# Low probability halves converted by VectorE, and gate work, stores and weight loads rescheduled, in a fused attention stage

## The chip, the cores and the metric

The kernel runs on one core of one Trainium2 chip. The metric is device time in microseconds of one execution, here the median of several runs. One execution was also recorded by the hardware profiler, and all durations below come from that one.

## The reference, cut to what matters

```python
z = einsum('bsd,de->bse', x, w_in) + b_in          # one projection, 2048 tokens x 1024
y_a = pool_mixer(za, ...) * silu(ga)
y_b = fox_attention(zq, zk, zv, zf) * silu(gb)     # 8 heads of 64, causal, forget-gate bias
y_c = s5_mixer(zc, ...) * silu(gc)
gates = sigmoid(zg)                                 # 3 x 1024 channels
merged = sum of gates[n] * (y_n @ w_up_n)
out = layer_norm(alpha * x + merged @ w_out)
# fox_attention, for each block of 128 queries:
logits = where(mask, q @ k.T * scale + F[t] - F[s], -inf)
y = softmax(logits) @ v
```

## The kernel before

Three stages follow each other: the input projections, scans and pooling; `stage_attend`; and the lifting and output projections. The change touches `stage_attend` alone, and the table `fill_plan` that it uses.

Products in this kernel are made of float32 operands split into a high part (rounded to the matmul's format) and a low part (the remainder); two or three matmuls then stand for one. `stage_attend` runs eight heads, one after the other, and mixes two kinds of work.

**Attention of a head**, by 16 tiles t of 128 queries. PE multiplies queries with all keys up to the tile's end into five PSUM banks `s_ps` (`queries`, L1819 and L1820). DVE subtracts the forget-gate row and takes the row maximum (`logits`, L1715, L1729). ACT makes the exponential (`weights_of`, L1636) and a float16 high half `p_hi` (`high_halves`, L1644); DVE makes the low half `p_lo` (L1783), in chunks of up to 1024 keys. A tile t of 8 or more has two chunks, so a head has 24. SP sends each half through a transposing DMA into `turn_hi` and `turn_lo` (L1467, L1471). ACT converts `turn_hi` to `pt_hi` (`high_turned`, L1649), POOL converts `turn_lo` to `pt_lo` (`low_turned`, L1534). PE then multiplies both with the values, two query tiles (a pair p) at a time (`values`, L1836), ACT copies half of the result (`low_rows`, L1607) and DVE adds it (`output`, L1738).

**Gates.** Beside that, PE computes the sigmoid gates for half of the tokens per four heads: each head has 6 weight tiles x 2 column chunks = 12 pieces of 24 matmuls (`fill`, L1866), 288 in all. Weight tiles come from HBM (L1392, issued by SP), are split by ACT (L1590) and DVE (L1699), the result goes through a tanh on ACT (`gates`, L1601) and is stored to `gateT` by SP (L1459).

What sets the order: each engine's program is written out by hand, with semaphores between them. `fill_plan` says how many of the 288 gate matmuls PE puts into each slot: "start" (ahead of or just behind the head's first query products), slot t behind the query products of tile t+1, "end" ahead of the last `values(7)`, and "tail" behind it. It also says in which slot a piece ends, and in which slot a weight tile is split. SP's queue holds the transposes of tile t and then the gate stores and weight loads of slot t; a wait there holds up all that stands behind it. POOL's queue holds the low-half conversions, the stores of each pair, and the loads of the next head: `load_kq` (four of 512 KB) at tile 15, `load_f` (1 MB), `load_v` (1 MB).

The lines that set the pace on PE before:

```python
for t in range(Q_TILES):
    if t + 1 < Q_TILES:
        queries(at, t + 1)
    fill(t)
    if t % 2 == 0 and t >= 2:
        values(at, t // 2 - 1, final)
fill("end")
values(at, 7, final)
fill("tail")
```

Of the kernel before, what the change touches and what calls it, by code (L numbers as in the profile page):

```python
# [1254 lines left out]
def fill_plan():  # L1255
# [32 lines left out]
FILL_START, FILL_END, FILL_TAIL, FILL_BASE = 30, 16, 22, 5  # L1288
# [16 lines left out]
def chunks_to(t):  # L1305

    return chunks(t)[-1][0] + 1


def stage_attend(nc, io, scr, kept, ident, mask, x_hi, x_lo, x_raw, gw_hi, gw_lo, gw_raw):  # L1310
# [4 lines left out]
    with ExitStack() as ctx:  # L1315
# [68 lines left out]
        assert nc.sbuf_base <= kept.wu_at + 4 * KT * KT * P  # L1384
        block = ctx.enter_context(nc.Block())

        @block.sync
        def _(sp):
            w_rows = io["w_tiles"].rearrange("m p (k c) -> (m p) k c", c=P)

            def load_w(first_row, par):
                sp.dma_start(gw_raw[par][:], w_rows[bass.ds(first_row, P)]).then_inc(gw_loaded[par], 16)  # L1392

# [5 lines left out]
            load_w((T_HALF + 1) * P, 1)  # L1399
# [38 lines left out]
            def body(phase, at, in_phase, last=False, turn=False):  # L1438
                now = (1 - phase) * HALF

                def gate_pieces(slot):
                    for piece in fill_ends[slot]:
# [19 lines left out]
                def transposes(t):  # L1462
                    for n, b0, nb in chunks(t):
# [3 lines left out]
                        sp.dma_start_transpose(turn_hi[n % 2][:, 0:nb, :], p_hi[n % 2][:, 0:nb * P]).then_inc(hi_turned[n % 2], 16)  # L1467
                        sp.wait_ge(p_low, at(CHUNKS_HEAD, n + 3))
# [4 lines left out]
                gate_pieces("start")  # L1473
                for t in range(Q_TILES):
# [3 lines left out]
                    gate_pieces(t)  # L1478
# [13 lines left out]
        def _(pool):  # L1492
# [33 lines left out]
            def low_turned(at, t):  # L1526

                if t >= 2 and t % 2 == 0:
                    pool.wait_ge(o_full, at(8, t // 2))
                    pool.sem_inc(passed)  # L1530
                for n, b0, nb in chunks(t):
                    pool.wait_ge(lo_turned[n % 2], at(CHUNKS_HEAD * 8, 16 * (n // 2) + (turned + 16)))
                    pool.sem_inc(passed)
                    pool.tensor_scalar(pt_lo[:, b0:b0 + nb, (t % 2) * P:(t % 2 + 1) * P], turn_lo[n % 2][:, 0:nb, :],  # L1534
                                       1.0 / HALVES, None, ALU.mult).then_inc(t_lo, 1)

            def tiles(at, row, last=False):
# [20 lines left out]
            with pool.Fori(0, HEADS - 1) as h:  # L1558
# [6 lines left out]
                low_turned(of_head, Q_TILES - 1)  # L1565
# [5 lines left out]
            low_turned(lambda k, c: (HEADS - 1) * k + c, Q_TILES - 1)  # L1571
# [14 lines left out]
        def _(act):  # L1586
# [5 lines left out]
            def gates(at, in_phase, slot, last=False):  # L1592
                for j in splits(slot, last):
                    split_w(at, j)
                for piece in fill_ends[slot]:
# [6 lines left out]
                                   bias=g_bias[:, bass.ds(in_phase(G_TILES, j), 1)]).then_inc(g_ready, 1)  # L1602

# [28 lines left out]
            def body(at, in_phase, last=False, turn=False):  # L1632
# [24 lines left out]
                gates(at, in_phase, "start", last)  # L1657
                for t in range(Q_TILES):
                    if t:
                        weights_of(t)  # L1660
                        if t % 2 and t >= 3:
                            low_rows(at, (t - 3) // 2)
                        before, now = chunks(t - 1), chunks(t)
# [799 lines left out]
```

## Time and profile before

| what | us |
|---|---|
| median of 3 runs (2101.03 to 2112.96) | 2109.07 |
| the profiled execution's own time | 2108.43 |
| its span | 2106.9 |
| PE busy in the span | 1825.6 (87%) |
| DVE, ACT, POOL busy | 1134.8, 833.9, 858.3 |
| DMA queue of SP, mean share of the 16 engines | 45.3% |
| DMA queue of POOL, the same | 11.4% |

Busy shares are means over stages with different limits. A row of a group tells the idle time of its engine just ahead of it and what ended that. PE's own durations overlap (matmuls are pipelined), so its pace is read from the distance between starts. The granted clock is given as a share of 2.4 GHz; 0.50 is 1.2 GHz.

### The profile page before, as it was taken

What the parts mean: (1) busy time and instruction counts of PE and PEld (TensorE: products, weight loads), DVE (VectorE), ACT (ScalarE), POOL (GpSimd) and SP (SyncE); (2) the same over time, 40 slices, a digit from 0 to 9 for tenths busy, and PEclk for the clock granted to TensorE, in tenths of its full rate; (3) what the DMA queues carried; (4) which work ended last, traced back from release to release, by engine and by line L of the source; (5) the groups of instructions that cost most, each with busy time, mean ns of one, the idle gap of its engine ahead of it and who ended that gap; (6) DMA issues with size and microseconds to landing.
All of it is one profiled execution on the core that took longest, in us unless ns stands there. A gap on an engine that the chain in (4) does not pass through costs nothing. (4 is left out here: it accounts for less than half of the span.)

```text
span 2106.9 us, 30302 instructions
## 1 busy us (share of the span) xinstructions
PE 1825.6 (87%) x9469; PEld 1556.6 (74%) x9469; DVE 1134.8 (54%) x2293; ACT 833.9 (40%) x1184; POOL 858.3 (41%) x778
## 2 busy tenths in 40 slices
PE   9999999999988689588596786886886889999998
PEld 7988888988866567566475565675665778999997
DVE  4555254653455346256264563462653658777766
ACT  3122131121255547356265564473663563121211
POOL 2919801990015425335155254253362451323232
PEclk9999999999999899789799898998998999999999
DMA  7322343323446747747668578477575788656652
GB/s 213 108 82 87 126 176 100 121 90 112 145 118 133 159 116 154 159 110 155 138 141 171 188 140 164 117 150 168 114 167 146 164 217 283 198 170 171 186 152 90
DMA packets 408628, 310.65 MB, mean 147 GB/s; under 512 B 304377, under 2 KB 354105, under 8 KB 405177
## 3 DMA queue, kind: packets, MB, share of 16 engines
q1 hardware_dynamic: 390576, 243.45, 45.3%
q0 software_dynamic: 15152, 63.06, 11.4%
q10 hardware_dynamic: 2800, 2.99, 0.6%
q8 instruction: 41, 0.67, 0.1%
q14 instruction: 59, 0.48, 0.1%
HBM read 164.05 MB, written 73.47 MB: 113 GB/s over the span
## 5 line engine op out<-in xcount | busy, mean ns | idle before, releaser
L1534 POOL TENSOR_SCALAR pt_lo<-turn_lo 128x1024 fp32r<-128x1024 f16 (+2 forms) x192 | 405.3, 2111 | 500.1 <-DMA turn_lo<-p_lo 411.8
L1836 PE MATMUL o_ps<-pt_hi,v_st 128*128 128x256 f32 x576 | 166.8, 319 | 224.0 <-POOL pt_lo L1534 208.2
L1836 PEld LDWEIGHTS o_ps<-pt_hi,v_st 128*128 128x128 f32 x576 | 128.6, 223 | 249.3 <-issue 249.2
L1866 PE MATMUL g_ps<-x_hi,w_hi 128*128 128x512 f32 x768 | 304.7, 397 | 0.0
L1866 PE MATMUL g_ps<-x_hi,w_lo 128*128 128x512 f32 x768 | 304.2, 396 | 0.0
L1715 DVE CUSTOM_DVE_ANT_0 s_sb<-s_ps,f_row 128x512 f32<-128x512 f32 (+3 forms) x288 | 160.1, 598 | 198.9 <-PE s_ps L1820 198.6
L1866 PE MATMUL g_ps<-x_lo,w_hi 128*128 128x512 f32 x768 | 233.0, 431 | 38.6 <-DVE w_lo L1699 37.4
L1783 DVE SCALAR_TENSOR_TENSOR p_lo<-s_sb,p_hi 128x1024 f16<-128x1024 f32 (+2 forms) x192 | 192.0, 1018 | 118.0 <-ACT p_hi L1644 111.6
L1866 PEld LDWEIGHTS g_ps<-x_lo,w_hi 128*128 128x128 f32 x768 | 157.4, 210 | 75.0 <-issue 32.4
L1649 ACT ACTIVATE pt_hi<-turn_hi 128x1024 fp32r<-128x1024 f16 (+2 forms) x192 | 154.1, 802 | 91.9 <-DMA turn_hi<-p_hi 91.8
L1636 ACT ACTIVATE s_sb<-s_sb,neg_max 128x128 f32<-128x128 f32 (+15 forms) x128 | 153.1, 1196 | 46.6 <-DVE neg_max L1729 46.4
L1866 PEld LDWEIGHTS g_ps<-x_hi,w_hi 128*128 128x128 f32 x768 | 148.1, 193 | 29.8
L1866 PEld LDWEIGHTS g_ps<-x_hi,w_lo 128*128 128x128 f32 x768 | 147.5, 192 | 29.9
L904 PE MATMUL tile_ps<-x_hi,w_hi 128*128 128x512 f32 x528 | 164.6, 393 | 0.2 <-DVE w_lo L511 0.2
L904 PE MATMUL tile_ps<-x_hi,w_lo 128*128 128x512 f32 x528 | 162.8, 389 | 0.0
L904 PE MATMUL tile_ps<-x_lo,w_hi 128*128 128x512 f32 x528 | 162.6, 389 | 0.0
L1836 PE MATMUL o_ps<-pt_lo,v_st 128*128 128x256 f32 x576 | 159.2, 313 | 0.0
L1699 DVE TENSOR_TENSOR w_lo<-w_lo_raw,w_hi 128x1024 fp32r<-128x1024 f32 x47 | 57.5, 1224 | 183.8 <-ACT w_hi L1590 183.8
L1644 ACT ACTIVATE p_hi<-s_sb 128x1024 f16<-128x1024 f32 (+2 forms) x192 | 151.7, 794 | 0.0
L2290 PE MATMUL u_ps<-y_hi,wu_hi 128*128 128x256 f32 x512 | 144.2, 282 | 4.2 <-DVE gate L2215 2.3
L2290 PE MATMUL u_ps<-y_lo,wu_hi 128*128 128x256 f32 x512 | 144.5, 282 | 0.0
L2290 PE MATMUL u_ps<-y_hi,wu_lo 128*128 128x256 f32 x512 | 143.8, 281 | 0.0
(333 smaller groups left out, 3845.3 us busy)
## 6 DMA issues: line engine op xcount, KB each, us to landing
w_lo_raw<-in_w_tiles SPq DMA_DIRECT2D x87, 512.0 KB, 4.2
gateT<-g_out SPq DMA_DIRECT2D x96, 256.0 KB, 4.2
gate<-gateT SPq DMA_DIRECT2D x62, 384.0 KB, 4.7
x_lo_raw<-in_xT SPq DMA_DIRECT2D x20, 512.0 KB, 9.7
vS<-v_out SPq DMA_DIRECT2D x32, 256.0 KB, 2.0
silT<-zout SPq DMA_DIRECT2D x16, 512.0 KB, 2.6
qkvT<-zout SPq DMA_DIRECT2D x16, 512.0 KB, 3.6
k_ll<-qkvT POOLq DMA_DIRECT2D x16, 512.0 KB, 8.1
```

Source lines behind the costliest of these rows:

```text
L904: last = pe.matmul(tile_ps[par][:, c * BANK:(c + 1) * BANK], w[par][:, k, :], x[:, k, c * BANK:(c + 1) * BANK], start=(k == 0 and j == 0), ...
L1534: pool.tensor_scalar(pt_lo[:, b0:b0 + nb, (t % 2) * P:(t % 2 + 1) * P], turn_lo[n % 2][:, 0:nb, :], 1.0 / HALVES, None, ALU.mult).then_inc ...
L1636: act.activation(row, row, ACT.Exp, bias=neg_max[t % 2][:], accum_out=row_sum[:, t:t + 1]).then_inc(p_ready, 1)
L1644: act.activation(p_hi[n % 2][:, 0:nb * P], s_sb[t % 2][:, b0 * P:(b0 + nb) * P], ACT.Copy, scale=HALVES).then_inc(p_high, 1)
L1649: act.activation(pt_hi[:, b0:b0 + nb, (t % 2) * P:(t % 2 + 1) * P], turn_hi[n % 2][:, 0:nb, :], ACT.Copy, scale=1.0 / HALVES).then_inc(t_h ...
L1699: dve.tensor_tensor(gw_lo[j % 2][:], gw_raw[j % 2][:], gw_hi[j % 2][:].bitcast(F32), ALU.subtract).then_inc(gw_split, 1)
L1715: return dve.tensor_tensor_reduce(s_sb[t % 2][:, k0 + a:k0 + b], s_ps[n % S_BANKS][:, a:b], f, 1.0, -3e38, ALU.subtract, ALU.max, mx[t % 2 ...
L1783: dve.scalar_tensor_tensor(p_lo[n % 2][:, 0:nb * P], s_sb[t % 2][:, b0 * P:(b0 + nb) * P], HALVES, p_hi[n % 2][:, 0:nb * P], ALU.mult, ALU ...
L1836: mm = pe.matmul(o_ps[:, 0, q], v_st[:, k, :], pt[:, k, q], start=(k == 0 and j == 0), stop=(k == last_key and j == 1))
L1866: mm = pe.matmul(g_ps[c][:], w[j % 2][:, k, :], x[:, k, c * BANK:(c + 1) * BANK], start=(r == 0), stop=(r == 3 * KT - 1))
L2290: mm = pe.matmul(u_ps[d % 2][:, n, :], w, y[:, k, :], start=(k == k0 and j == 0), stop=(k == k1 - 1 and j == 2))
```

## The change

1. `low_turned` moves from POOL to DVE. It is done one tile later, chunk by chunk: in the iteration of tile t, DVE converts chunk i of tile t-1 behind `p_lo` of chunk i of tile t. POOL keeps only DMAs.
2. ACT makes `high_halves` of tile t ahead of `high_turned` of tile t-1, and the tanh of slot t-1 moves into the iteration of tile t, behind the exponential.
3. The weight loads are issued by ACT, behind the tanh of the piece that frees the buffer, in place of SP. Weight splits stand in the middle of a tile, behind its first chunk; at the head's end they stand behind the split of the next head's keys and queries.
4. SP stores the gates of slot t-1 between the first high and the first low transpose of tile t.
5. PE starts `values(p)` behind `queries` of tile 2p+4 in place of behind `fill` of tile 2p+2, and does all products with `pt_hi` first; it waits for `t_lo` only ahead of those with `pt_lo`.
6. The gate matmuls of a head are 14 (start), 8, 10, 10, 11, 12, 13, 13, 14, 15, 15, 16, 17, 18, 18, 20, 20 (slots 0 to 15), 30 (end), 14 (tail). Before: 30, then 5, 7, 7, 9, 10, 11, 12, 13, 15, 15, 17, 17, 19, 20, 21, 22, then 16 and 22.

```diff
-FILL_START, FILL_END, FILL_TAIL, FILL_BASE = 30, 16, 22, 5
+FILL_START, FILL_END, FILL_TAIL, FILL_BASE = 14, 30, 14, 12
-                at = s + (3 if s < 4 else 2)
+                at = s + (3 if s < 12 else 2)
...
@@ SP, transposes(t)
-                    for n, b0, nb in chunks(t):
+                    for i, (n, b0, nb) in enumerate(chunks(t)):
...
                         sp.dma_start_transpose(turn_hi[n % 2][:, 0:nb, :], p_hi[n % 2][:, 0:nb * P]).then_inc(hi_turned[n % 2], 16)
+                        if i == 0:
+                            gate_pieces(t - 1 if t else "start")
...
@@ ACT, body
+                for t in range(1, Q_TILES):
+                    weights_of(t)
+                    gates(at, in_phase, t - 1, last, turn)
+                    before = chunks(t - 1)
+                    for i, part in enumerate(chunks(t)):
+                        high_halves(t, *part)
+                        if i == 0:
+                            if t % 2 and t >= 3:
+                                low_rows(at, (t - 3) // 2)
+                            for j in splits(t, last):
+                                split_w(at, j)
+                        if i < len(before):
+                            high_turned(t - 1, *before[i])
...
@@ DVE
+            def low_turned(at, t, n, b0, nb):
+                dve.wait_ge(lo_turned[n % 2], at(CHUNKS_HEAD * 8, 16 * (n // 2) + (turned + 16)))
+                dve.sem_inc(passed)
+                dve.tensor_scalar(pt_lo[:, b0:b0 + nb, (t % 2) * P:(t % 2 + 1) * P], turn_lo[n % 2][:, 0:nb, :],
+                                  1.0 / HALVES, None, ALU.mult).then_inc(t_lo, 1)
...
@@ DVE, body, behind p_lo of chunk i of tile t
+                        if i == 0:
+                            if t % 2 and t >= 3:
+                                output(at, (t - 3) // 2, last)
+                            for j in splits(t, last):
+                                split_w(at, j)
+                        if i < len(before):
+                            low_turned(at, t - 1, *before[i])
...
@@ PE, values
-                for part in (t_hi, t_lo):
-                    pe.wait_ge(part, at(CHUNKS_HEAD, chunks_to(2 * p + 1) + 2))
+                pe.wait_ge(t_hi, at(CHUNKS_HEAD, chunks_to(2 * p + 1) + 2))
...
+                for j, pt in enumerate((pt_hi, pt_lo)):
+                    if j:
+                        pe.wait_ge(t_lo, at(CHUNKS_HEAD, chunks_to(2 * p + 1) + 2))
...
@@ PE, head
+                        if t % 2 and t >= 3:
+                            values(at, (t - 3) // 2, final)
                         fill(t)
-                        if t % 2 == 0 and t >= 2:
-                            values(at, t // 2 - 1, final)
```

DVE at the end of a head, in the kernel before (`pt_lo` does not occur on it):

```order
572 L1783 SCALAR_TENSOR_TENSOR p_lo<-s_sb,p_hi 128x1024
573 L1780 REGISTER_ALU
574 L1783 SCALAR_TENSOR_TENSOR p_lo<-s_sb,p_hi 128x1024
575 L1787 RECIPROCAL row_inv<-row_sum 128x16
576 L1698 REGISTER_ALU
577 L1699 TENSOR_TENSOR w_lo<-w_lo_raw,w_hi 128x1024
```

The same place in the kernel after:

```order
592 L1779 SCALAR_TENSOR_TENSOR p_lo<-s_sb,p_hi 128x1024
593 L1730 REGISTER_ALU
594 L1731 REGISTER_ALU
595 L1733 TENSOR_TENSOR y_out_108<-o_ps,o_low 64x256
596 L1687 REGISTER_ALU
597 L1688 TENSOR_TENSOR w_lo<-w_lo_raw,w_hi 128x1024
598 L1724 TENSOR_SCALAR pt_lo<-turn_lo 128x8x128
599 L1776 REGISTER_ALU
600 L1779 SCALAR_TENSOR_TENSOR p_lo<-s_sb,p_hi 128x1024
601 L1724 TENSOR_SCALAR pt_lo<-turn_lo 128x7x128
602 L1790 RECIPROCAL row_inv<-row_sum 128x16
603 L1722 REGISTER_ALU
```

The conversions of tile 14 now stand between and behind the two `p_lo` of tile 15; the pair's sum and a weight split stand ahead of the first of them.

PE around `values(1)`, before (four key tiles; `s_ps` are the query products that follow):

```order
1812 L1826 REGISTER_ALU
1813 L1830 ISA
1814 L1836 MATMUL o_ps<-pt_hi,v_st 128x256
1815 L1836 MATMUL o_ps<-pt_lo,v_st 128x256
1816 L1836 MATMUL o_ps<-pt_hi,v_st 128x256
1817 L1836 MATMUL o_ps<-pt_lo,v_st 128x256
...
1822 L1817 REGISTER_ALU
1823 L1819 MATMUL s_ps<-k_hh,q_st 128x512
1824 L1820 MATMUL s_ps<-k_ll,q_st 128x512
```

After:

```order
1809 L1820 MATMUL s_ps<-k_hh,q_st 128x512
1810 L1821 MATMUL s_ps<-k_ll,q_st 128x512
...
1816 L1838 MATMUL o_ps<-pt_hi,v_st 128x256 x3
1817 L1838 MATMUL o_ps<-pt_hi,v_st 128x128
1818 L1838 MATMUL o_ps<-pt_lo,v_st 128x256 x3
1819 L1838 MATMUL o_ps<-pt_lo,v_st 128x128
1820 L1868 MATMUL g_ps<-x_hi,w_lo 128x512
```

The next tile's query products have moved ahead of the value products, and the high ones stand ahead of the low ones.

SP at the end of a head, before:

```order
249 L1467 DMA_TRANSPOSE turn_hi<-p_hi 128x8x128
250 L1468 REGISTER_ALU
251 L1471 DMA_TRANSPOSE turn_lo<-p_lo 128x8x128
252 L1467 DMA_TRANSPOSE turn_hi<-p_hi 128x8x128
253 L1468 REGISTER_ALU
254 L1471 DMA_TRANSPOSE turn_lo<-p_lo 128x8x128
255 L1392 ISA
256 L1392 DMA w_lo_raw<-in_w_tiles 128x1024
```

After:

```order
237 L1461 DMA_TRANSPOSE turn_hi<-p_hi 128x8x128
238 L1452 REGISTER_ALU
239 L1453 ISA
240 L1453 DMA gateT<-g_out_106 128x512
241 L1464 REGISTER_ALU
242 L1467 DMA_TRANSPOSE turn_lo<-p_lo 128x8x128
243 L1461 DMA_TRANSPOSE turn_hi<-p_hi 128x8x128
244 L1464 REGISTER_ALU
245 L1467 DMA_TRANSPOSE turn_lo<-p_lo 128x8x128
```

A gate store now stands ahead of the first low transpose of tile 15, and the weight load has left the queue.

## Rows read from the trace of the kernel before

**Rows 1.** Windows by stage: stretch, length, busy by engine, clock, DMA share, GB/s
```profile
0.00:595.00 595.00, 588.22 (x3056) 498.00 (x3056) 299.48 (x336) 128.11 (x150) 283.45 (x378) 1.00 0.37 122
595.00:1735.00 1140.00, 878.46 (x4106) 731.65 (x4107) 563.62 (x1454) 626.15 (x897) 476.00 (x306) 0.89 0.67 150
1735.00:2106.90 371.90, 358.95 (x2309) 326.95 (x2307) 271.73 (x504) 79.66 (x138) 98.81 (x94) 0.99 0.60 180
```

**Rows 2.** Groups by line: busy us, mean ns of one, idle before, releaser
```profile
L1534 POOL TENSOR_SCALAR pt_lo<-turn_lo 128x1024 fp32r<-128x1024 f16 (+2 forms) x192 | 405.3, 2111 | 500.1 <-DMA turn_lo<-p_lo 411.8 <-PE o_ps L1836 83.1
...
L1866 PE MATMUL g_ps<-x_lo,w_hi 128*128 128x512 f32 x768 | 233.0, 431 | 38.6 <-DVE w_lo L1699 37.4 <-PEq L1891 1.2
...
L1836 PE MATMUL o_ps<-pt_hi,v_st 128*128 128x256 f32 x576 | 166.8, 319 | 224.0 <-POOL pt_lo L1534 208.2 <-issue 15.8
```

**Rows 3.** PE's timeline, one head: all its rows that begin behind a wait
```profile
907.89 0.58 PE L1836 MATMUL o_ps<-pt_hi,v_st 128*128 128x256 f32 x1 [6.65 <-POOL pt_lo L1534]
927.55 0.57 PE L1836 MATMUL o_ps<-pt_hi,v_st 128*128 128x256 f32 x1 [2.67 <-POOL pt_lo L1534]
941.09 0.38 PE L1836 MATMUL o_ps<-pt_hi,v_st 128*128 128x256 f32 x1 [0.22 <-POOL pt_lo L1534]
955.58 0.38 PE L1836 MATMUL o_ps<-pt_hi,v_st 128*128 128x256 f32 x1 [2.37 <-POOL pt_lo L1534]
971.34 0.38 PE L1836 MATMUL o_ps<-pt_hi,v_st 128*128 128x256 f32 x1 [1.65 <-POOL pt_lo L1534]
988.26 0.38 PE L1836 MATMUL o_ps<-pt_hi,v_st 128*128 128x256 f32 x1 [0.86 <-POOL pt_lo L1534]
998.82 3.65 PE L1866 MATMUL g_ps<-x_lo,w_hi 128*128 128x512 f32 x8 [4.21 <-DVE w_lo L1699]
1024.15 0.58 PE L1836 MATMUL o_ps<-pt_hi,v_st 128*128 128x256 f32 x1 [17.55 <-POOL pt_lo L1534]
```

**Rows 4.** PE's timeline at full clock: gate matmuls, sixteen starts
```profile
597.16 0.40 PE L1866 MATMUL g_ps<-x_hi,w_hi 128*128 128x512 f32 x1
...
600.57 0.39 PE L1866 MATMUL g_ps<-x_hi,w_lo 128*128 128x512 f32 x1
```

**Rows 5.** `turn_lo` in 990 to 1025 us, and windows in that head's end
```profile
DMA to landing us min/median/max: 2.9/3.3/22.5
...
1000.00:1005.00 5.00, 5.00 (x19) 4.02 (x18) 0.00 (x0) 1.06 (x1) 3.91 (x4) 0.78 1.00 209
...
1015.00:1020.00 5.00, 0.00 (x0) 0.00 (x0) 0.00 (x0) 0.00 (x0) 0.00 (x0) 0.50 1.13 88
```

**Rows 6.** Windows: the head of Rows 3, from key split to key split
```profile
878.70:1025.60 146.90, 110.72 (x515) 92.48 (x515) 67.72 (x178) 77.34 (x110) 58.63 (x39) 0.86 0.65 140
```

**Rows 7.** POOL's and SP's timelines around the end of that head
```profile
997.95 0.56 POOL L1495 DMA_DIRECT2D k_ll<-qkvT  x1
...
1000.57 0.58 POOL L1502 DMA_DIRECT2D f_row<-fcum  x1
...
1021.15 2.76 POOL L1534 TENSOR_SCALAR pt_lo<-turn_lo 128x1024 fp32r<-128x1024 f16 x1 [17.16 <-DMA turn_lo<-p_lo]
...
998.50 1.23 SPq L1471 DMA_TRANSPOSE turn_lo<-p_lo  x1
```

**Rows 8.** Groups by form: conversions on three engines
```profile
L1534 POOL TENSOR_SCALAR pt_lo<-turn_lo 128x1024 fp32r<-128x1024 f16 x80 | 224.3, 2804 | 274.7 <-DMA turn_lo<-p_lo 194.3 <-PE o_ps L1836 79.7
L771 DVE TENSOR_SCALAR m_in<-zf 8x2048 f32<-8x2048 f32 x1 | 1.2, 1206 | 0.0
L691 DVE TENSOR_SCALAR pool_u<-tile_ps,bias 128x1024 f32<-128x1024 f32 x4 | 5.1, 1284 | 9.8 <-PE tile_ps L904 9.8
```

**Rows 9.** DVE's timeline, tile 15 of that head: first logits, first low half of tile 14
```profile
981.53 0.69 DVE L1715 CUSTOM_DVE_ANT_0 s_sb<-s_ps,f_row 128x512 f32<-128x512 f32 x1 [0.73 <-PE s_ps L1820]
...
984.52 1.23 DVE L1783 SCALAR_TENSOR_TENSOR p_lo<-s_sb,p_hi 128x1024 f16<-128x1024 f32 x1
```

**Rows 10.** A DMA issued by ACT's queue
```profile
25.31 0.34 ACTq L258 DMA_DIRECT2D vb_lo_raw<-in_w_vf  x1
```

More of the change, by code:

```diff
@@ L1477, in body @@
                     transposes(t)
-                    gate_pieces(t)
+                gate_pieces(Q_TILES - 1)
                 if last:
@@ L1590, in split_w, with gates @@
                 act.activation(gw_hi[j % 2][:], gw_raw[j % 2][:], ACT.Copy).then_inc(gw_split_hi, 1)
-            def gates(at, in_phase, slot, last=False):
-                for j in splits(slot, last):
-                    split_w(at, j)
+            def gates(at, in_phase, slot, last=False, turn=False):
                 for piece in fill_ends[slot]:
@@ L1602, in gates @@
                                    bias=g_bias[:, bass.ds(in_phase(G_TILES, j), 1)]).then_inc(g_ready, 1)
+                    if c == NCH - 1 and not (last and j + 2 >= G_TILES):
+                        if turn and j + 2 >= G_TILES:
+                            load_w(act, (T_HALF + j + 2 - G_TILES) * P, j % 2)
+                        else:
+                            load_w(act, in_phase(G_TILES * P, (T_HALF + j + 2) * P), j % 2)
             def low_rows(at, p):
@@ L1656, in body @@
                     high_halves(0, *part)
[L1657 to L1663, printed above, removed]
-                        for i in range(len(now)):
-                            if i < len(before):
-                                high_turned(t - 1, *before[i])
-                            high_halves(t, *now[i])
-                    gates(at, in_phase, t, last)
+                gates(at, in_phase, "start", last, turn)
+                for t in range(1, Q_TILES):
[11 more added lines that the diff above has]
+                            high_turned(t - 1, *before[i])
+                gates(at, in_phase, Q_TILES - 1, last, turn)
                 for part in chunks(Q_TILES - 1):
@@ L1676, in body @@
                         high_wu(i)
-                gates(at, in_phase, "end", last)
+                else:
+                    split_kq(at(64, 128))
+                for j in splits("end", last):
+                    split_w(at, j)
+                gates(at, in_phase, "end", last, turn)
                 if last:
@@ L1688, in body @@
                     high_x(0)
-                gates(at, in_phase, "tail", last)
+                gates(at, in_phase, "tail", last, turn)
                 if turn:
@@ L1778, in body @@
                         logits(at, t + 1)
-                    for n, b0, nb in chunks(t):
+                    before = chunks(t - 1) if t else []
+                    for i, (n, b0, nb) in enumerate(chunks(t)):
                         dve.wait_ge(p_high, at(CHUNKS_HEAD, n + 1))
@@ L1787, in body @@
                         dve.reciprocal(row_inv[:, 0:t + 1], row_sum[:, 0:t + 1]).then_inc(inv_ready, 1)
-                    for j in splits(t, last):
-                        split_w(at, j)
-                    if t % 2 and t >= 3:
-                        output(at, (t - 3) // 2, last)
-                for j in splits("end", last):
-                    split_w(at, j)
+                for part in chunks(Q_TILES - 1):
+                    low_turned(at, Q_TILES - 1, *part)
                 if last:
@@ L1799, in body @@
                     split_kq(at(2, 4))
+                for j in splits("end", last):
+                    split_w(at, j)
                 output(at, 7, last)
@@ L1831, in values @@
                 last_key = 2 * p + 1
-                for k in range(last_key + 1):
-                    q = slice(P, 2 * P) if k == last_key else slice(0, 2 * P)
-                    for j, pt in enumerate((pt_hi, pt_lo)):
+                for j, pt in enumerate((pt_hi, pt_lo)):
+                    if j:
+                        pe.wait_ge(t_lo, at(CHUNKS_HEAD, chunks_to(2 * p + 1) + 2))
+                    for k in range(last_key + 1):
+                        q = slice(P, 2 * P) if k == last_key else slice(0, 2 * P)
                         mm = pe.matmul(o_ps[:, 0, q], v_st[:, k, :], pt[:, k, q], start=(k == 0 and j == 0),
```

30 lines of the change are left out of this document (5 added, 25 removed).

## The prediction

> **What bounds the kernel now.** First I read the windows by stage [rows 1]. Ahead of 595 us and behind 1735 us PE is busy 588.2 of 595.0 and 359.0 of 371.9 us at a clock of 1.00 and 0.99: the change touches neither, and there is nothing for it to win. In the attention stage between them PE is busy 878.5 of 1140 us at a mean clock of 0.89. So 261.5 us are idle, 32.7 in each of the eight heads, and a head takes 142.5. The groups by line then say what ends that idle time: value products waiting for POOL's conversion of the low halves, 224.0 us in all, and gate products waiting for a weight split, 37.4 [rows 2]. PE's timeline of one head shows where [rows 3]: 6.7 us ahead of the first value product, 0.2 to 2.7 ahead of the next five, 4.2 ahead of the gate products of the last weight tile, and 17.6 ahead of the last value product. That is 32.0 of waits for low halves in this head; the mean over the heads is 224.0 / 8 = 28, so the others are like it and somewhat shorter, above all in the last wait (the last head loads nothing for a next one).
>
> How much work is in a head? 15 steps between gate matmuls of 512 columns take 3.41 us, 0.227 each [rows 4]. So 288 of them are 65.5 us. The query products have 136 x 128 keys twice, 34,816 columns, and the value products 128 x 256 + 16 x 128, as many: at the gates' pace per column 15.4 us each. Together 96.3 us at full clock. PE is busy 878.5 / 8 = 109.8, so 13.5 us a head are lost to the low clock: behind long waits it is granted 0.50 [rows 5], and the eight gate matmuls behind the wait at 998.82 take 3.65 us [rows 3] in place of 8 x 0.227 = 1.8. **A head is 96.3 work + 13.5 slow clock + 32.7 idle.** No other engine is near: in a head of 146.9 us DVE is busy 67.7, ACT 77.3, POOL 58.6 [rows 6].
>
> POOL is named as releaser, but it was itself waiting for the transposing DMA, 411.8 us [rows 2]. At the head's end it issued the loads of the next head's keys and queries (2 MB) from 997.95 and the gate row (1 MB) at 1000.57. SP issued the last low transpose at 998.50, and it landed after 22.5 us, where the median is 3.3; the DMA engines were fully busy meanwhile [rows 5, 7]. So of the 17.6 us POOL's own arithmetic is 2.8, and the rest is that collision. This wait is half of a head's idle time, and what becomes of it decides the size of the result.
>
> **The change, part by part.**
>
> *The conversion on DVE.* POOL takes 2.80 us for 1024 keys [rows 8]. The trace has no such operation on DVE. Nearest is a one-operand instruction with both tiles in SBUF, 2048 in 1.21 us (0.59 ns per column); an upper bound is one that reads PSUM, 1024 in 1.28 (1.25 ns) [rows 8]. A head has 17,408 columns: 10.3 to 21.8 us. I take 12, by the row it is like. DVE goes to 67.7 + 12 = 80 us a head, 90 at worst: below PE's 96. For the last pair of chunks 2 x 2.8 us on POOL become 2 x 0.7.
>
> *First value product, 6.7 us.* The chain from the first row maximum to the converted tile 1 loses POOL's small conversions and a store that stood ahead of the first transpose, but stays some 9 us of exponential, halves and transposes. Ahead of it PE now has 28 gate matmuls in place of 19 (8 + 10 + 10 for 5 + 7 + 7), +2.0 us, and the query products of tile 4, +0.6. I leave 3, bounds 1 and 6.
>
> *The next ones up to pair 6*, 7.8 us in this head. Queries of the next tile now stand ahead of the wait, so DVE gets its input while PE waits, and half of the products (those with `pt_hi`) need no low half. Between the query products of an even tile and the values PE has 1.8 + 4.5 + 1.8 us late in the head (0.227 x 2 per 512 keys, 20 gate matmuls); DVE needs 3.0 (logits) [rows 9], 2.4 (two `p_lo` of 1.23 at most) and 1.4 (conversions). That fits, with 1 to 2 us over. I leave 2, bounds 0 and 8.
>
> *Weight splits, 4.2 us.* The last tile's split comes earlier in tile 15, and PE reaches it with matmul 240, late in slot 15. But tile 3's split now stands in tile 10 and PE wants it 9 matmuls into that slot, where DVE has logits and a `p_lo` ahead of it: 2 us, bounds 0 and 4. ACT issues 6 loads a head, 0.34 us each [rows 10]: 2 us on an engine that has 60 free. SP loses them, and loses their wait for PE.
>
> *Last value product, 17.6 us (some 14 in a mean head).* Two effects, opposed. POOL no longer lags, so it issues the 2 MB as soon as tile 15's query products are done, about 14 us earlier: those were done by 981.53, where DVE starts on tile 15 [rows 9]. They then run beside the transposes of tile 14 and the first of tile 15, and the 1 MB beside the rest. The sum of bytes is the same, and a load begun 14 us earlier ends that much earlier; but more transposes are in its way. From the start of tile 15's query products PE now has these 1.8, 20 gate matmuls 4.5, `values(6)` 3.2, again 20 gates 4.5 and the 30 of "end" 6.8: 21 us. The chain needs: 2 MB at 209 GB/s [rows 5] 10 us (from +2), then tile 15's halves and transposes, an estimate of 10 (three landings of 3.3), and the 1 MB 5: about +28. Before, the last values began 42 us behind that point. I leave 7, bounds 0 and 15. The Trainium skill, page "DMA: Bandwidth & Descriptors", section "Queues, rings and completion order", says that each DMA engine takes turns between queues packet by packet. This trace agrees as far as it goes: the one transpose that shared the DMA engines with POOL's loads took 22.5 us to land, 19 more than the median. By it the early load would slow four to six transposes, not two, and the wait would stay: the first rival below.
>
> *Slow clock.* Of four to five waits over 2 us a head, two stay. 13.5 becomes 7, bounds 2 and 11.
>
> *Reordering of ACT, SP stores a tile later, and the even spread of gates* cost nothing by themselves: the work is the same, and ACT at 79 and SP's queue stay below PE: that work hides them. If PE came near 100 us a head this cover would be thin, since DMA work is 0.65 x 146.9 = 95 us a head [rows 6].
>
> Sum: 96.3 + 3 + 2 + 2 + 7 + 7 = 117.3 us a head, 25.2 less than 142.5. Eight heads give 202 us. The last head has no load of a next head to collide with and so less to win; I take off 8: 194. From the profiled execution's 2108.4 us: **1914 us**. That execution lies 0.6 below the median of the runs, so no correction.
>
> **The rivals.**
>
> *A. The collision stays.* The wait at the head's end keeps 15 us and the clock loss 9: 127.3 + 1 for thinner cover, 128.3 a head, 14.2 x 8 = 114 less, 1994 us. For it: the landing of 22.5 us and DMA at 1.00 to 1.13 [rows 5]. Against it: the loads start earlier, and 12 to 14 more gate matmuls stand ahead.
>
> *B. DVE becomes the bound late in the head.* If the conversion costs 1.28 per 1024, tiles 10 to 15 need some 8 us of DVE each (3.0 + 2.4 + 2.5), with a weight split over that, and DVE holds the pace: 1.3 us for each of six tiles, +8 a head, 1978 us. For it: the order, a landing now waited for by DVE with the next logits queued behind. Against: DVE's total of 90 at worst.
>
> *C. Slower: two serial landings.* DVE and ACT now wait in order for tile 14's transposes between the two chunks of tile 15. If tile 14's transposes crawl under the 2 MB load (19 us more than 3.3) and then tile 15's under the 1 MB and the stores (19 us more), the chain holds two collisions in place of one: a wait of 15 + 19, clock 12: 96.3 + 3 + 2 + 2 + 34 + 12 = 149.3 a head, +6.8, 2162 us. It decides if the two delays together exceed some 33 us. Against: DMA work of all those bytes is about 30 us, so both can't be full.
>
> *D. No gain.* POOL's lag was harmless and each wait returns with another releaser, within 0.5% (10 us, about what a measurement of this kernel can tell from no change): 2108. Against: the conversion is 2.8 us of every wait, and PE's order alone removes some.
>
> *E. Nearly all goes.* Wait at the end 2, first 1, others 1, clock 4: 96.3 + 8 = 104.3 a head, 38 less in each of seven and 12 in the last, 1830 us, since the load ends before PE gets there.
>
> **How the numbers follow.** Forecast 0.48, A 0.19, B 0.10, E 0.14, C 0.05, D 0.04. Faster: 0.91, same 0.04, slower 0.05. The range 1835 to 2025 holds the forecast with its bounds, A and B with 30 us over, and half of E; it leaves out C, D and the rest of E.
>
> **What would show it.** In the new profile POOL has no busy group in the stage; the conversion on DVE is 0.6 to 0.8 us for 1024 keys (B: 1.2 or more). PE's busy time in the stage falls from 878 to about 830, the clock rises to 0.93 or more, and idle time from 262 to about 110. The wait ahead of the last value product is 4 to 10 us (A: 13 or more, C: 25 or more) and is ended by DVE's conversion behind a landing. The row of the last weight tile's wait is gone, and a smaller one may stand in slot 10. The forecast is wrong if PE's waits between pairs 1 and 6 grow, or if key loads lengthen the landings of tile 14 so that the last wait keeps its length.

## The result, and the profile after

The changed kernel takes 1989.3 us (median of three, 1986.6 to 2016.0), against 2109.1 before: a ratio of 0.948, interval 0.934 to 0.961. It is faster by 120 us, where 194 were forecast (1914 us); the range held it. Since its own three runs span 29 us, a difference of 20 us to it is read below together with the traces. The profiled execution has a span of 1985.0 us against 2106.9, 121.9 less.

The attention stage in the windows of the kernel after; the columns are those of [rows 1]:

```profile
596.00:1614.00 1018.00, 857.02 (x4109) 715.56 (x4109) 649.37 (x1646) 635.69 (x898) 74.63 (x114) 0.93 0.76 168
```

All the gain is here: 1140 us became 1018, 127.3 a head. PE's busy time fell from 878.5 to 857.0 (about 830 were forecast) and its idle time from 261.5 to 161.0 (110 were forecast). POOL is all but empty, DVE grew from 564 to 649.

The groups by line, the answer to [rows 2]:

```profile
L1868 PE MATMUL g_ps<-x_lo,w_hi 128*128 128x512 f32 x768 | 230.9, 430 | 95.3 <-DVE w_lo L1688 91.4
...
L1779 DVE SCALAR_TENSOR_TENSOR p_lo<-s_sb,p_hi 128x1024 f16<-128x1024 f32 (+2 forms) x192 | 175.1, 912 | 115.2 <-DMA turn_lo<-p_lo 97.1
...
L1628 ACT ACTIVATE p_hi<-s_sb 128x1024 f16<-128x1024 f32 (+2 forms) x192 | 154.0, 802 | 132.8 <-DMA turn_hi<-p_hi 123.1
...
L1838 PE MATMUL o_ps<-pt_hi,v_st 128*128 128x256 f32 x576 | 80.2, 285 | 47.9 <-ACT pt_hi L1633 47.9
```

The value products waited 224.0 us before and now 57 (47.9, and 9.3 ahead of the low ones). The wait for weight splits grew from 37.4 to 91.4 and is now the largest. And two waits are new: ACT's high half and DVE's low half wait for the landing of the transpose that frees their buffer, 123.1 and 97.1 us. ACT's high half did not wait before. DVE's low half stood idle as long, but for ACT:

```profile
L1783 DVE SCALAR_TENSOR_TENSOR p_lo<-s_sb,p_hi 128x1024 f16<-128x1024 f32 (+2 forms) x192 | 192.0, 1018 | 118.0 <-ACT p_hi L1644 111.6 <-issue 1.8
```

PE's timeline of one head, the answer to [rows 3], with all rows that begin behind a wait:

```profile
865.45 0.68 PE L1838 MATMUL o_ps<-pt_hi,v_st 128*128 128x256 f32 x2 [5.60 <-ACT pt_hi L1633]
866.78 0.69 PE L1838 MATMUL o_ps<-pt_lo,v_st 128*128 128x256 f32 x2 [0.65 <-DVE pt_lo L1724]
907.13 2.36 PE L1868 MATMUL g_ps<-x_lo,w_hi 128*128 128x512 f32 x7 [3.01 <-DVE w_lo L1688]
931.70 2.11 PE L1868 MATMUL g_ps<-x_lo,w_hi 128*128 128x512 f32 x8 [1.51 <-DVE w_lo L1688]
943.16 1.88 PE L1838 MATMUL o_ps<-pt_lo,v_st 128*128 128x256 f32 x14 [0.44 <-DVE pt_lo L1724]
955.33 3.78 PE L1868 MATMUL g_ps<-x_lo,w_hi 128*128 128x512 f32 x8 [6.56 <-DVE w_lo L1688]
966.55 2.12 PE L1838 MATMUL o_ps<-pt_hi,v_st 128*128 128x256 f32 x16 [1.24 <-ACT pt_hi L1633]
974.44 2.10 PE L1868 MATMUL g_ps<-x_lo,w_hi 128*128 128x512 f32 x8 [0.56 <-DVE w_lo L1688]
```

The waits of pairs 1 to 6 are all but gone, and the last one fell from 17.6 to 1.2. In their place stand the splits of weight tile 3 (3.0), 4 (1.5) and, above all, 5 (6.6). In the seven heads that load for a next one, the wait for tile 5's split is 2.5 to 12.2 us.

Around that last split, on POOL, SP, ACT and DVE:

```profile
937.28 0.52 POOL L1490 DMA_DIRECT2D k_ll<-qkvT  x1 [5.00 <-PE s_ps L1821]
...
940.60 9.01 SPq L1467 DMA_TRANSPOSE turn_lo<-p_lo  x1
...
951.11 1.06 ACT L1628 ACTIVATE p_hi<-s_sb 128x1024 f16<-128x1024 f32 x1 [8.53 <-DMA turn_hi<-p_hi]
...
952.52 1.23 DVE L1779 SCALAR_TENSOR_TENSOR p_lo<-s_sb,p_hi 128x1024 f16<-128x1024 f32 x1 [9.42 <-DMA turn_lo<-p_lo]
...
954.00 1.21 DVE L1688 TENSOR_TENSOR w_lo<-w_lo_raw,w_hi 128x1024 fp32r<-128x1024 f32 x1
...
964.49 0.69 DVE L1724 TENSOR_SCALAR pt_lo<-turn_lo 128x1024 fp32r<-128x1024 f16 x1 [6.39 <-DMA turn_lo<-p_lo]
```

The 2 MB load begins at 937.28, right behind tile 15's query products. From there tile 14's transposes crawl: SP needs 9.01 us to issue one of them (1.2 else), and ACT and DVE stand still for 8.5 and 9.4 us. The weight split is behind them in DVE's order, so PE, which does not need the transposes for another 11 us, waits for the split. **The collision at the head's end is still there; it moved from tile 15's transposes to tile 14's, and its stall reaches PE by another way.** That the load is its cause is shown by the first experiment below.

The conversion by form on DVE:

```profile
L1724 DVE TENSOR_SCALAR pt_lo<-turn_lo 128x1024 fp32r<-128x1024 f16 x80 | 54.9, 687 | 65.1 <-DMA turn_lo<-p_lo 65.0
...
L1724 DVE TENSOR_SCALAR pt_lo<-turn_lo 128x896 fp32r<-128x896 f16 x16 | 17.2, 1072 | 0.0
```

1024 keys take 0.69 us, as taken in the sum. All 192 take 117.6 us, 14.7 a head; 12 were forecast, and the odd sizes like 896 make the difference.

### The profile page after: what moved, and what is told of

It is laid out like the page before. It is cut to its first block and busy times, and to the rows that moved or that the text cites. A ratio compares the mean times of both kernels' runs of the same rounds, so it can differ in the third digit from the quotient of the medians.

```text
span 1985.0 us, 30017 instructions
## 1 busy us (share of the span) xinstructions
PE 1805.1 (91%) x9469; PEld 1542.0 (78%) x9469; DVE 1223.3 (62%) x2485; ACT 842.4 (42%) x1184; POOL 455.8 (23%) x586
## 3 DMA queue, kind: packets, MB, share of 16 engines
q0 software_dynamic: 15152, 63.06, 12.0%
## 5 line engine op out<-in xcount | busy, mean ns | idle before, releaser
L1868 PE MATMUL g_ps<-x_lo,w_hi 128*128 128x512 f32 x768 | 230.9, 430 | 95.3 <-DVE w_lo L1688 91.4
L1868 PE MATMUL g_ps<-x_hi,w_hi 128*128 128x512 f32 x768 | 310.4, 404 | 0.0
L1868 PE MATMUL g_ps<-x_hi,w_lo 128*128 128x512 f32 x768 | 308.7, 402 | 0.0
L1779 DVE SCALAR_TENSOR_TENSOR p_lo<-s_sb,p_hi 128x1024 f16<-128x1024 f32 (+2 forms) x192 | 175.1, 912 | 115.2 <-DMA turn_lo<-p_lo 97.1
L1511 POOL DMA_DIRECT2D mixT<-y_out x63 | 40.1, 636 | 852.5 <-DVE y_out L1733 698.7
L1628 ACT ACTIVATE p_hi<-s_sb 128x1024 f16<-128x1024 f32 (+2 forms) x192 | 154.0, 802 | 132.8 <-DMA turn_hi<-p_hi 123.1
L1724 DVE TENSOR_SCALAR pt_lo<-turn_lo 128x1024 fp32r<-128x1024 f16 (+2 forms) x192 | 117.6, 613 | 106.9 <-DMA turn_lo<-p_lo 106.5
L1868 PEld LDWEIGHTS g_ps<-x_hi,w_hi 128*128 128x128 f32 x768 | 149.3, 194 | 30.3
L375 ACT ACTIVATE w_hi<-w_lo_raw 128x1024 fp32r<-128x1024 f32 x39 | 41.3, 1058 | 195.1 <-DMA w_lo_raw<-in_w_tiles 195.1
L1838 PE MATMUL o_ps<-pt_hi,v_st 128*128 128x256 f32 x576 | 80.2, 285 | 47.9 <-ACT pt_hi L1633 47.9
L1820 PE MATMUL s_ps<-k_hh,q_st 128*128 128x512 f32 (+2 forms) x320 | 120.1, 376 | 3.9 <-DVE q_st L1750 2.7
```

The source lines that it names most:

```text
L1628: act.activation(p_hi[n % 2][:, 0:nb * P], s_sb[t % 2][:, b0 * P:(b0 + nb) * P], ACT.Copy, scale=HALVES).then_inc(p_high, 1)
L1724: dve.tensor_scalar(pt_lo[:, b0:b0 + nb, (t % 2) * P:(t % 2 + 1) * P], turn_lo[n % 2][:, 0:nb, :], 1.0 / HALVES, None, ALU.mult).then_inc( ...
L1779: dve.scalar_tensor_tensor(p_lo[n % 2][:, 0:nb * P], s_sb[t % 2][:, b0 * P:(b0 + nb) * P], HALVES, p_hi[n % 2][:, 0:nb * P], ALU.mult, ALU ...
L1820: pe.matmul(ps, q_st[:, t * P:(t + 1) * P], k_hh[:, k0:k0 + keys], start=True, stop=False)
L1838: mm = pe.matmul(o_ps[:, 0, q], v_st[:, k, :], pt[:, k, q], start=(k == 0 and j == 0), stop=(k == last_key and j == 1))
L1868: mm = pe.matmul(g_ps[c][:], w[j % 2][:, k, :], x[:, k, c * BANK:(c + 1) * BANK], start=(r == 0), stop=(r == 3 * KT - 1))
```

## The experiments

Each was run beside the kernel before on the same chip; its ratio is to that kernel. The theory has three parts. The 2 MB load collides with whichever transposes are in flight. A weight split that PE waits for costs what that wait shows. The place of the value products and the engine of the conversion share the gain. Rivals are in each expectation. Parts 2 and 4 of the change (ACT's order and the later stores of the gates) and the place of the splits within a tile (part 3) were not taken out by themselves.

| run | us | ratio to before, interval |
|---|---|---|
| the change | 1989.3 | 0.948, 0.934 to 0.961 |
| e1 split a slot earlier | 1968.3 | 0.933, 0.930 to 0.937 |
| e2 key load later | 2007.0 | 0.951, 0.948 to 0.953 |
| e3 key load tiny | 1931.2 | 0.914, 0.911 to 0.917 |
| e4 last split early | 1988.4 | 0.943, 0.939 to 0.947 |
| e5 old fill counts and split slots | 1969.7 | 0.932, 0.928 to 0.937 |
| e6 conversion on POOL | 2051.2 | 0.972, 0.965 to 0.978 |
| e7 old value order | 2048.7 | 0.970, 0.966 to 0.973 |
| e8 before, conversion on DVE | 2074.6 | 0.981, 0.978 to 0.985 |
| e9 e1, head split later | 1962.7 | 0.929, 0.926 to 0.932 |
| e10 e1, queries loaded early | 1999.5 | 0.944, 0.941 to 0.948 |
| e11 e9 and e10 | 1992.9 | 0.942, 0.939 to 0.946 |
| e12 weights loaded by SP | 2000.9 | 0.946, 0.943 to 0.950 |

### The load at the head's end

```diff
@@ e3, load_kq (q_st alike)
-pool.dma_start(k_ll[half], scr["qkvT"][q_row + D_B ...])
+pool.dma_start(k_ll[half, 0:P], scr["qkvT"][q_row + D_B ..., 0:P])
```

> The change, but of the next head's keys and queries only 128 columns are loaded (128 KB in place of 2 MB), so heads 1 to 7 work on wrong keys and queries. Theory: the landings of tile 14's transposes return to 3 us, DVE and ACT do not stall, the wait at the last weight tile falls from 6.5 to under 1, that of the last value product stays under 3: 7 x 9 = 63 us less than the change, about 1922. Rival (DVE's own order at the end sets that wait): within 15 us of the change, and the row of the last weight tile's wait stays over 4 us.

1931.2 us: 58 less than the change (63 expected). DVE's timeline of this run at tile 15's first low half, then PE's at the last value product:

```profile
929.65 1.23 DVE L1779 SCALAR_TENSOR_TENSOR p_lo<-s_sb,p_hi 128x1024 f16<-128x1024 f32 x1 [2.10 <-DMA turn_lo<-p_lo]
```
```profile
945.55 3.67 PE L1838 MATMUL o_ps<-pt_hi,v_st 128*128 128x256 f32 x16 [4.15 <-ACT pt_hi L1633]
```

DVE's stall there fell from 9.4 to 2.1 us and the row of the last weight tile's wait is gone, as expected; the last wait did not stay under 3, it is 4.2. The gate row's 1 MB is still loaded while tile 15's transposes are in flight; whether it makes this wait was not tested. So the 2 MB load costs 8 us in each of seven heads, and the theory holds against DVE's order as the cause.

```diff
@@ e2: load_kq from tile 15's start to just ahead of load_f
-                        load_kq(row + HD)
+                pool.wait_ge(s_full, h * S_PIECES + S_PIECES)
+                load_kq(h * HD + HD)
                 pool.wait_ge(s_free, h * S_PIECES + S_PIECES)
                 load_f(h + 1)
```

> The change, but the 2 MB of keys and queries of the next head are loaded behind the store of pair 6, together with the gate row, some 17 us later. Theory (the 2 MB crawl over whichever transposes are in flight): the wait of 6.5 us at the last weight tile goes to under 1, DVE's stall of 9 us on tile 14's landing goes, and the wait of the last value product grows from 1.5 to 12 to 16; 7 x 5 = 35 us slower than the change, about 2020. Rival (where the load stands does not matter, bytes are bytes): within 10 us of the change. Second rival (the early load is a loss of its own): 30 us or more faster.

2007.0 us, 18 more than the change by the medians (35 expected); the intervals overlap (0.948 to 0.953 and 0.934 to 0.961). PE's timeline of this run, the last value product, and the landings of its low transposes:

```profile
848.42 3.67 PE L1837 MATMUL o_ps<-pt_hi,v_st 128*128 128x256 f32 x16 [12.83 <-ACT pt_hi L1632]
```
```profile
DMA to landing us min/median/max: 2.2/3.0/30.3
```

The wait is back in its old place, 12.8 us, and the longest landing is 30.3. In the seven heads that load, this wait is 14.8 us on average; in the change, the wait for tile 5's split and the last one are 8.8 together. Over the profiled executions PE is idle for 207.8 us here and 179.9 in the change. So the traces show the early load of the change as the better of the two places, though neither is free; by the times alone that is not settled.

```diff
@@ e4, fill_plan
-                at = s + (3 if s < 12 else 2)
+                at = s + (1 if s == 13 else 3 if s < 12 else 2)
```

> The change, but the last weight tile (5) is split in slot 14 in place of 15. Theory (the chain of transposes to the last value product is what counts, and the wait at the weight tile only stands in its shadow): the 6.5 us wait at the weight tile goes and the wait of the last value product grows by about as much, to 7 to 8; time within 10 us of the change. Rival (the weight split is itself the limit): 7 x 6 = 42 us less, about 1945.

1988.4 us, the change's time, as expected. PE's timeline of this run:

```profile
961.25 2.12 PE L1868 MATMUL g_ps<-x_lo,w_hi 128*128 128x512 f32 x8 [1.74 <-ACT g_out L1580]
...
971.61 3.58 PE L1838 MATMUL o_ps<-pt_hi,v_st 128*128 128x256 f32 x16 [7.77 <-ACT pt_hi L1633]
```

The 6.6 us at the weight tile became 1.7 (now behind ACT's stalled tanh) and the last value product's 1.2 became 7.8. The largest row of the profile after was a shadow: what counts there is when tile 15's transposes land.

```diff
@@ e10: load_kq keeps k_ll and the last quarter of q_st; POOL, behind the store of a pair
+                        if t in (5, 9, 13) and not last:
+                            pool.wait_ge(s_full, at(S_PIECES, pieces_to(t)))
+                            load_q(row + HD, t // 4 - 1)
```

> As e1, and three quarters of the next head's queries are loaded at tiles 5, 9 and 13, where their columns are free, so that 1.25 MB in place of 2 MB are loaded at tile 15. Theory (the price of that load is in proportion to what is loaded beside tile 14's transposes; all of it costs 54 us by e3): 0.75 / 2 of 54 = 20 us less than e1, 1948, with shorter waits at value product 6 and 7. Rival (the same bytes cost the same wherever they meet transposes): within 6 us of e1.

1999.5 us: 31 more than e1, where 20 less were expected. This misses the theory's forecast that the price goes by the bytes at tile 15. DVE's timeline of this run, late in a head:

```profile
939.65 1.23 DVE L1787 SCALAR_TENSOR_TENSOR p_lo<-s_sb,p_hi 128x1024 f16<-128x1024 f32 x1 [3.14 <-DMA turn_lo<-p_lo]
...
947.13 1.09 DVE L1787 SCALAR_TENSOR_TENSOR p_lo<-s_sb,p_hi 128x896 f16<-128x896 f32 x1 [5.65 <-DMA turn_lo<-p_lo]
...
968.05 0.69 DVE L1732 TENSOR_SCALAR pt_lo<-turn_lo 128x1024 fp32r<-128x1024 f16 x1 [10.24 <-DMA turn_lo<-p_lo]
```

The quarter at tile 13 begins 2.3 us ahead of the rest, and the stall is spread over three chunks and is no shorter. The price does not go by bytes at tile 15. The run also has more packets on POOL's queue for the same 63.06 MB (16,720 for 15,152), since rows are cut in four; whether the cut rows or the earlier start made it slower was not told apart. e11 adds the head split of e9 to it:

> e9 and e10 together. Theory: the two are at different places of the head and add up, 35 us less than e1, 1933. Rival: less than half of that, 1950 or more.

1992.9 us: more than e9 alone (1962.7) and within 7 us of e10, so its rival (1950 or more) holds and the two do not add up.

### The splits and the counts

```diff
@@ e1, fill_plan
-                at = s + (3 if s < 12 else 2)
+                at = s + (3 if s < 4 else 2)
```

> The change, but the weight tiles 3, 4 are split in slots 9 and 12, as in the kernel before, in place of 10 and 13. Theory (PE paces tiles 2 to 13 and waits there only for these splits): the waits of 3.0 and 1.3 us a head at the gate products of tiles 3 and 4 go, with some slow clock, 8 x 4.5 = 36 us less than the change, about 1953. Rival (DVE paces these tiles, so that the time returns in another wait, or the weight load has not landed and ACT waits for it): within 10 us of the change.

1968.3 us, 21 less than the change (36 expected); all four runs (1960.3 to 1975.9) lie below the change's three. PE's timeline of this run, tiles 9 to 15 of a head: the rows of the weight tiles 3 and 4 are gone, and

```profile
942.08 3.25 PE L1838 MATMUL o_ps<-pt_lo,v_st 128*128 128x256 f32 x14 [4.55 <-DVE pt_lo L1724]
950.25 2.11 PE L1868 MATMUL g_ps<-x_lo,w_hi 128*128 128x512 f32 x8 [0.24 <-DVE w_lo L1688]
962.05 3.67 PE L1838 MATMUL o_ps<-pt_hi,v_st 128*128 128x256 f32 x16 [3.79 <-ACT pt_hi L1633]
```

PE now reaches the collision earlier and gives part back there: 4.6 and 3.8 us, 8.6 in all with the split, where the change had 8.2. That the time fell shows that PE does pace the tiles up to 13, and the rival (DVE paces them) falls.

```diff
@@ e5
-FILL_START, FILL_END, FILL_TAIL, FILL_BASE = 14, 30, 14, 12
+FILL_START, FILL_END, FILL_TAIL, FILL_BASE = 30, 16, 22, 5
-                at = s + (3 if s < 12 else 2)
+                at = s + (3 if s < 4 else 2)
```

> The change with the old counts of gate matmuls (30 at the start, 16 end, 22 tail, steep in between) and the old slots of the splits. Theory (the even spread gives PE work ahead of the first and the last value product, where the chain of transposes ends late): the wait of the first value product grows by 2 us, that of the last by 3 to 8 (14 gate matmuls fewer ahead of it, and no wait at the weight tile to hide in), less 20 us for the splits as seen when they alone were a slot earlier: 15 to 50 us slower than the change, about 2015. Rival (the counts only shift idle time): within 10 us of the change, or faster by the 20 us of the splits.

1969.7 us: 20 less than the change, and the time of e1, which has the same split slots with the new counts. The theory falls and the rival's second form holds: with the old split slots the even spread of the gate products is worth nothing that can be measured. PE's groups of this run show why:

```profile
L1868 PE MATMUL g_ps<-x_lo,w_hi 128*128 128x512 f32 x768 | 229.9, 426 | 40.2 <-DVE w_lo L1688 35.7 <-ACT g_out L1580 2.4 <-PEq L1893 1.2
L1838 PE MATMUL o_ps<-pt_lo,v_st 128*128 128x256 f32 x576 | 91.8, 311 | 36.3 <-DVE pt_lo L1724 36.3
L1838 PE MATMUL o_ps<-pt_hi,v_st 128*128 128x256 f32 x576 | 89.0, 306 | 60.0 <-ACT pt_hi L1633 60.0
```

The three waits are 132 us; in e1 the same three are 130 (8.0 + 40.7 + 81.2). The counts only decide on which of them the collision falls.

```diff
@@ e9, fill_plan, on top of e1
-    splits["head"] = [1]
+    splits["head"], splits[1] = [], [1]
```

> As e1 (splits of tiles 3, 4 a slot earlier), and the split of weight tile 1 stands in slot 1 in place of the head's first steps, where it lies between the first and the second logits. Theory (the wait ahead of the first value product, 3.5 us in a mean head of e1 with its low part, is the chain exponential, halves, transposes of tiles 0 and 1, and 2.8 us of it are this split on ACT and DVE): 1.5 to 2.8 us a head less, 1950 against e1's 1968. Rival (SP's issue of the first transpose, or the landing, sets it): within 6 us of e1.

1962.7 us, 6 less than e1, which is what the rival allows, and the intervals overlap (0.926 to 0.932 and 0.930 to 0.937). The theory's 12 to 22 us did not come. PE's timeline, the first value product of a head, first of e1, then of e9:

```profile
986.00 0.44 PE L1838 MATMUL o_ps<-pt_hi,v_st 128*128 128x256 f32 x2 [2.52 <-ACT pt_hi L1633]
987.48 0.45 PE L1838 MATMUL o_ps<-pt_lo,v_st 128*128 128x256 f32 x2 [1.04 <-DVE pt_lo L1724]
```
```profile
975.33 0.44 PE L1838 MATMUL o_ps<-pt_hi,v_st 128*128 128x256 f32 x2 [2.77 <-ACT pt_hi L1633]
976.83 0.66 PE L1838 MATMUL o_ps<-pt_lo,v_st 128*128 128x256 f32 x2 [1.06 <-DVE pt_lo L1724]
```

In this head nothing changed. Over all heads the waits for `pt_hi` fell from 81.2 to 62.1 us, but the profiled execution of e9 is its fastest (1944.5), 18 us below its median, so this fall is no typical one. Whether this split is part of the wait at all is left open. e9 is the fastest version of the study that computes everything, and beats the change: its interval ends at 0.932, the change's begins at 0.934.

### What the gain is made of

```diff
@@ e6: low_turned back to POOL, with its old place and its old wait for o_full; DVE without it
@@ e7, PE
-                        if t % 2 and t >= 3:
-                            values(at, (t - 3) // 2, final)
                         fill(t)
+                        if t % 2 == 0 and t >= 2:
+                            values(at, t // 2 - 1, final)
@@ and in values: high and low in turn, both waits ahead of them
```

> The change, but the conversion of the low halves is done by POOL again, as in the kernel before (and POOL's loads stand behind it). Theory (the engine of the conversion matters less than the order; POOL needs 2.8 us for 1024 keys, DVE 0.7, and POOL's lag also keeps the 2 MB load back to where it hits tile 15): waits of 2 to 4 us at value products 1 to 6 and over 10 at the last: 2050, half of the change's gain. Rival A (the conversion is nearly all of it): over 2090. Rival B (the order is all of it): under 2005.

2051.2 us, 62 more than the change. POOL's timeline of this run, then PE's:

```profile
962.50 0.57 POOL L1490 DMA_DIRECT2D k_ll<-qkvT  x1
...
983.64 2.76 POOL L1529 TENSOR_SCALAR pt_lo<-turn_lo 128x1024 fp32r<-128x1024 f16 x1 [14.19 <-DMA turn_lo<-p_lo]
```
```profile
983.81 3.67 PE L1848 MATMUL o_ps<-pt_hi,v_st 128*128 128x256 f32 x16 [15.60 <-ACT pt_hi L1647]
```

Waits for POOL at value products are only 27 us in this run. The slow conversion hurts chiefly in another way: PE has made tile 15's query products by 948.6, but POOL's load begins only at 962.5, when tile 15's transposes are in flight, and the last wait is 15.6 again. In the seven heads that load, the last waits are 106 us here and 13 in the change, which in turn waits 49 for tile 5's split: 44 more, of 55 that PE is idle more in the whole execution.

> The change, but PE does its value products where they stood before (behind fill of tile 2p+2, ahead of the query products of tile 2p+4), high and low in turn, and waits for both halves first. Theory (the query products ahead of the wait feed DVE): DVE waits for query products again, PE waits 1 to 2 us at each of pairs 1 to 6: 8 x 4 to 6 = 30 to 50 us slower than the change, about 2025. Rival (with a fast conversion the place is indifferent): within 10 us of the change.

2048.7 us, 59 more than the change; 36 were expected. The waits of this run:

```profile
DVE s_sb L1704 <- PE s_ps L1821: 193.8, 68, 5.5
...
PE o_ps L1837 <- DVE pt_lo L1724: 102.3, 48, 11.8
```

In the change DVE waits 82.9 us for query products, and PE at value products 57.2 for high and low halves together. This run undoes three things at once (the place of the value products, high ahead of low, and the later wait for the low halves); together they are worth as much as the engine of the conversion, and how they share it was not told apart.

```diff
@@ e8: the kernel before; low_turned on DVE in the change's place (with output of a pair ahead of it), none on POOL
```

> The kernel before with one part of the change alone: DVE converts the low halves, a tile later, in the change's place on DVE; all else as before. Theory (the parts need each other: PE's old order asks for the low half of tile 2p+1 one fill earlier than DVE now gives it): waits ahead of pairs 1 to 6 stay at 1.5 to 3, the last one loses POOL's 2.8 and its load stands earlier: 2070, a third of the gain. Rival (the conversion's engine is nearly all): 2010 or less. Second rival: no gain, 2100 or more, since DVE's landing waits now hold back the logits.

2074.6 us, 35 less than before: 2070 was expected. PE's timeline, the last value product and the gate products behind it:

```profile
984.54 0.58 PE L1833 MATMUL o_ps<-pt_hi,v_st 128*128 128x256 f32 x1 [5.83 <-DVE pt_lo L1721]
...
1000.31 3.53 PE L1863 MATMUL g_ps<-x_lo,w_hi 128*128 128x512 f32 x8 [7.13 <-DVE w_lo L1685]
```

The last wait is shorter, 5.8, but a weight split behind it is now waited for 7.1, so part of the old 17.6 has only moved here too; and the waits of pairs 1 to 6 stay at 0.9 to 2.0. Alone the conversion gives 35 us, on top of all the rest of the change 62 (e6): the parts need each other.

```diff
@@ e12: load_w issued by SP behind its wait for g_ready, none on ACT
```

> The change, but SP issues the weight loads again, behind the wait for the tanh. Theory (the issuing queue matters only at the end, where a weight load on SP's queue stands behind transposes that crawl under the 2 MB load): the waits at the last weight tile grow by 0 to 3 us, time 0 to 20 us more than the change, about 1995. Rival (one queue for each kind is what made the weight loads land): over 2010, with waits at weight tiles 2 to 4 too. Second rival: no difference.

2000.9 us, 12 more than the change by the medians. The intervals (0.943 to 0.950 and 0.934 to 0.961) do not separate them, and the kernel before, run beside e12, itself took 4 us more (2113.3) than beside the change. So the second rival, no difference, stands. PE's waits for splits grew from 91.4 to 103.8 us:

```profile
PE g_ps L1868 <- DVE w_lo L1688: 103.8, 26, 8.1
```

By the medians, the parts taken out of the change one by one give: conversion 62, order of the value products 59, weight loads 12 (not told from none), counts 0, and the new split slots cost 20. Such prices need not add up, and the parts that were not taken out are not among them.

## Why the prediction was right, and where not

Its direction, its main mechanism and its range held; its time was 75 us too low. By its steps, a head forecast at 117.3 us against 127.3 measured (eighths of the stage's sums; the slow clock is PE's busy time less the 96.3 of work):

| term | forecast | measured |
|---|---|---|
| first value product | 3 | 5.1 |
| pairs 1 to 6 | 2 | 0.5 |
| weight splits | 2 | 11.4 |
| last value product | 7 | 1.6 |
| other | 0 | 1.5 |
| slow clock | 7 | 10.8 |

*The conversion on DVE* was right: 0.69 us for 1024, taken by the one-operand row in SBUF, and DVE at 81 us a head against 80. That DVE's sum came out so close is part luck: the conversions took 14.7 a head for 12, and the low halves, 24.0 a head before, took 21.9, which the working did not see.

*The order* was right for pairs 1 to 6, and e7 shows that it is worth 59 us, 7.4 a head, where its term was 5.8 (7.8 less 2).

*The weight splits* are the step that failed. Their wait was bounded at 0 to 4 us. They measured 11.4 us a head. Tile 3's was seen and under-priced (2 for 3.5), tile 4's forgotten (1.6), and tile 5's was thought gone, "late in slot 15", where it measured 6.1: the working looked at DVE's busy time there and not at the landing that DVE and ACT wait for just ahead of the split. Rival C named that very wait in order; the sum did not carry it into the split behind it. Together with the last value product, whose term was 7, the collision was forecast at 7 and measured at 6.1 + 1.6 = 7.7: e4 shows that the two are one wait, and e3 that the load's price is 8 us a head. From the start of tile 15's query products to the last value product 32 us pass in the head shown, where the chain was put at 28. So the size of the collision was about right and its place wrong.

What was missed in size is then tile 3 and 4's splits (5.1 for 2; e1: 21 us in all), the first value product (5.1 for 3) and the slow clock (10.8 for 7). The working kept two waits over 2 us a head; 28 are left in the eight heads, 3.5 a head. Eight gate matmuls behind the 6.6 us wait take 3.78 us, much as behind the 4.2 us wait before (3.65, [rows 3]).

*The even spread* was costed at nothing by itself but used as cover for the first and last value product. e5 shows no cover that can be measured.

*Rival A* (1994 us) has the measured time, but not its rows: its wait of 15 us at the last value product is 1.6, or 7.7 with the split that now stands ahead of it. The page "DMA: Bandwidth & Descriptors" of the Trainium skill, "Queues, rings and completion order", says that an engine takes turns between queues packet by packet. The runs agree in that tile 14's transposes crawl once POOL's load runs (9.4 us of stall with it, 2.1 without, e3); that the turns are taken by packets none of them shows. That by this the wait would stay whole was wrong: in the seven heads that load it was 14.5 us before, and 8.8 now with the split.

*Rival B* did not come: pairs 1 to 6 wait 0.5 us. *C* did not come: 9.4 and 6.4 us of stall in series in the head shown, not 19 and 19. *D* and *E* did not come; e3 shows that without the 2 MB load the kernel would still take 1931.

## What to carry to other kernels

When a wait is ended by a DMA that shares the engines with a bulk load, moving the load moves the wait to whatever is then in flight, and behind an in-order engine it may surface at an instruction that has nothing to do with it. Before pricing a wait at nothing, list what stands ahead of the awaited instruction in its engine's order and what each of those waits for. And before fixing the largest row of a profile, ask whether it is only a shadow: moved away in e4, it came back in full two steps later, while of the two small ones (3.0 and 1.5 us) more than half was real: 21 of 36 us.

## What the runs showed of the hardware that was not expected

The conversion on DVE is fast for an even number of 128-key blocks and slow for an odd one: 1024 keys 0.69 us, but 896 keys 1.07 us; 768 keys 0.55, but 640 keys 0.81. Why was not tried.

Issuing a transposing DMA takes SP 1.2 us (median), but 9.0 while POOL's load is running (11.2 at most), so a crawling transpose also holds up what stands behind it in SP's queue.

Between 937.3 and 951.1 us, while ACT and DVE stood still for a landing, the windows of the change show the DMA engines full and the rate no higher than in [rows 5]:

```profile
937.30:951.10 13.80, 11.04 (x61) 9.22 (x59) 4.33 (x11) 5.28 (x7) 2.04 (x4) 1.00 1.01 209
```

DVE makes the low halves quicker when POOL does not compute beside it, here before and after:

```profile
L1783 DVE SCALAR_TENSOR_TENSOR p_lo<-s_sb,p_hi 128x1024 f16<-128x1024 f32 x80 | 108.7, 1358 | 80.0 <-ACT p_hi L1644 75.6
L1779 DVE SCALAR_TENSOR_TENSOR p_lo<-s_sb,p_hi 128x1024 f16<-128x1024 f32 x80 | 98.0, 1224 | 101.6 <-DMA turn_lo<-p_lo 96.9 <-issue 1.0 <-ACT p_hi L1628 0.2
```

With the conversion alone moved off POOL (e8) it is 1.22 us too, and with it back on POOL (e6) 1.30.
